# The opening of a two-layer trunk kernel: the first tile scaled behind its transpose, three requests and one rounding in another order

## What is computed

```
def rms_norm(x, g):
    y = x * lax.rsqrt(jnp.mean(x * x, axis=-1, keepdims=True) + EPS)
    return y * g

for l in range(DEPTH):
    h = rms_norm(x, norm_g[l])
    proj = jnp.einsum('bsd,de->bse', h, w_in[l])
    (a_u, a_v, a_z, b_q, b_k, b_v, b_z, i_q, i_k, i_w, g_a, g_b) = split_columns(proj)
    ...
    qi = apply_rope(i_q.reshape(b, s, IDX_HEADS, IDX_DIM), cos_i, sin_i)
    ki = apply_rope(i_k[:, :, None, :], cos_i, sin_i)[:, :, 0, :]
    ...
```

## Time and profile before

| | us |
|---|---|
| median of 3 runs | 775.14 (774.41 to 775.39) |
| the profiled execution | 773.44 |
| its span, first to last instruction | 771.6 |
| TensorE / DVE / ScalarE busy | 762.0 / 620.5 / 460.7 |

### The profile page before, as it was taken

How to read it: one execution, slowest core, us unless ns; L and a number is a source line. 1 busy time by engine, 2 the same in 40 slices (tenths; PEclk the granted TensorE clock), 3 DMA queues, 4 the chain that set the end, 5 groups by cost and what they waited for, 6 DMA issues and landing times.

```text
span 771.6 us, 12228 instructions
## 1 busy us (share of the span) xinstructions
PE 762.0 (99%) x4364; PEld 666.3 (86%) x4364; DVE 620.5 (80%) x1051; ACT 460.7 (60%) x866; POOL 131.5 (17%) x125
## 2 busy tenths in 40 slices
PE   7999999999999999999999999999999999999998
PEld 7988878888899889988899788888889998999886
DVE  5767999999978884689986689999998878746895
ACT  5578786442577556735665977664335684676342
POOL 1344111000030103012215420300011101210130
PEclk9999999999999999999999999999999999999999
DMA  9838558522695529495874745893248844665784
GB/s 330 289 73 200 130 117 227 183 85 83 164 205 148 133 68 156 137 273 127 192 242 148 173 106 149 172 263 110 67 87 221 179 158 69 123 136 181 203 151 122
DMA packets 57900, 123.10 MB, mean 160 GB/s; under 512 B 3824, under 2 KB 8112, under 8 KB 57840
## 3 DMA queue, kind: packets, MB, share of 16 engines
q0 software_dynamic: 23568, 50.42, 34.6%
q1 hardware_dynamic: 33984, 71.31, 28.3%
q10 hardware_dynamic: 288, 0.59, 0.2%
HBM read 107.63 MB, written 10.49 MB: 153 GB/s over the span
## 4 chain that ended last, share of the span: by engine, by line
PE 89%; DVE 4%; ACT 4%; issue 2%; DMA 1%; ACTq 0%; DVEq 0%
PE bank L950 11%; PE bank L952 11%; PE bank L951 11%; PE bank L1020 7%; PE bank L1021 7%; PE bank L1019 7%; PE bank L1103 6%; PE bank L989 3%; PE bank L987 3%; PE bank L988 3%; PE bank L1048 3%; PE bank L1049 3%; PE bank L1050 3%; PE bank L924 2%; PE bank L942 2%
## 5 line engine op out<-in xcount | busy, mean ns | idle before, releaser
L1618 DVE TENSOR_TENSOR w_lo<-w_raw,w_hi 128x1024 fp32r<-128x1024 f32 x168 | 203.1, 1220 | 30.3 <-ACT w_hi L1190 25.4
L1190 ACT ACTIVATE w_hi<-w_raw 128x1024 fp32r<-128x1024 f32 x168 | 172.9, 1052 | 43.4 <-DMA w_raw<-in_w_out 18.9
L783 POOL DMA_DIRECT2D w_raw<-in_w_in x48 | 57.5, 1211 | 396.2 <-DVE w_lo L1618 371.5
L1019 PE MATMUL bank<-h_hi,w_lo 128*128 128x256 f32 x256 | 75.6, 295 | 0.0
L950 PE MATMUL bank<-h_lo,w_hi 128*128 128x512 f32 x192 | 75.5, 393 | 0.0
L952 PE MATMUL bank<-h_hi,w_hi 128*128 128x512 f32 x192 | 74.8, 389 | 0.0
L951 PE MATMUL bank<-h_hi,w_lo 128*128 128x512 f32 x192 | 74.7, 389 | 0.0
L1021 PE MATMUL bank<-h_hi,w_hi 128*128 128x256 f32 x256 | 72.4, 283 | 0.0
L1020 PE MATMUL bank<-h_lo,w_hi 128*128 128x256 f32 x256 | 72.4, 283 | 0.0
L1019 PE MATMUL bank<-hs,w_lo 128*128 128x256 f32 x192 | 56.3, 293 | 0.0
L1698 DVE MAX8 top<-score 128x8 f32<-128x256 f32 (+2 forms) x96 | 53.5, 558 | 3.4 <-DVE g_a L1863 1.8
(11 more groups left out here) (239 smaller groups left out, 1960.9 us busy)
## 6 DMA issues: line engine op xcount, KB each, us to landing
w_raw<-in_w_in SPq DMA_DIRECT2D x84, 512.0 KB, 4.5
w_raw<-in_w_in POOLq DMA_DIRECT2D x48, 512.0 KB, 6.7
w_raw<-in_w_out POOLq DMA_DIRECT2D x16, 512.0 KB, 6.7
w_raw<-in_w_out SPq DMA_DIRECT2D x12, 512.0 KB, 4.3
out<-x_sb POOLq DMA_DIRECT2D x4, 1024.0 KB, 5.8
w_raw<-in_w_oa SPq DMA_DIRECT2D x8, 512.0 KB, 3.7
w_raw<-in_w_ob SPq DMA_DIRECT2D x8, 512.0 KB, 4.1
x_sb<-out POOLq DMA_DIRECT2D x2, 2048.0 KB, 10.9
```

What stands on the lines that cost most here:

```text
L783: pool.dma_start(w_raw[:, slot], block_weights(layer, u), accum_op=ALU.add) \
L1019: nc.tensor.matmul(dst, w_lo[:, wk, col], a_hi[:, k], start=first and i == 0, stop=False, skip_group_check=True)
L1190: nc.scalar.activation(hi, w_raw[:, raw_slot(layer, u)], ACT.Copy).then_inc(s_whi.sem, 1)
L1618: nc.vector.tensor_tensor(lo, w_raw[:, raw_slot(layer, u)], hi.bitcast(F32), ALU.subtract) \
```

## The change

The first tile of layer 0 is no longer multiplied by the norm gain before its transpose. DVE multiplies it by the reciprocal root alone, in two halves with a signal each. The gain stands, transposed, in eight new columns beside the identity matrix (eye_g, whose load grows from 128 to 136 columns) and is applied behind the transpose, where a column of it is a scale per partition: in ScalarE's rounding, now four activations of 128 columns for each half, and in DVE's remainder, four instructions for each half. These transposes go to banks 1 to 4, two blocks in each, and the products of the first tile wait for each k step's remainder alone. norm_bc is requested by ScalarE behind the first tile's root instead of at its start. SP requests the second x tile behind unit 2 instead of ahead of it. POOL requests the rope tables and gains when the second xn is written. ScalarE rounds unit 2 ahead of the second tile's statistics, and DVE takes unit 2's remainder ahead of the second xn and the second half of h_lo ahead of the small weights. In layer 0 the second tile's transposes move from k = 4 to k = 6 of the first tile's products. WARM_UP goes from 18 to 14. In layer 1 only POOL's request is moved.

```diff
@@ constants
-WARM_UP = 18
+WARM_UP = 14
-X_AFTER = {2: [1], 4: [2], 5: [3]}
+X_AFTER = {3: [1], 4: [2], 5: [3]}
@@ tiles
-        eye = sb("eye", [P, P])
+        eye_g = sb("eye_g", [P, P + KD])
+        eye, g_col = eye_g[:, 0:P], eye_g[:, P:P + KD]
@@ POOL
-                pool.wait_ge(s_xn.sem, s_xn.at(layer, 1))
+                pool.wait_ge(s_xn.sem, s_xn.at(layer, 2))
                 pool.dma_start(rope[:], rope_cs).then_inc(s_rope.sem, 16)
@@ TensorE, transpose_x
-                pe.wait_ge(s_xn.sem, s_xn.at(layer, t + 1))
+                first = layer == 0 and t == 0
+                if not first:
+                    pe.wait_ge(s_xn.sem, s_xn.at(layer, t + 1))
...
-                    dst = bank[3 + 2 * (t % 2) + half]
+                    if first:
+                        pe.wait_ge(s_xnhalf, half + 1)
                     for k in range(4):
                         kk = 4 * half + k
-                        last = nc.tensor.transpose(dst[:, k * P:(k + 1) * P], xn[:, t % 2, kk * P:(kk + 1) * P], eye[:])
+                        if first:
+                            dst, col = bank[1 + kk // 2], k % 2 * P
+                        else:
+                            dst, col = bank[3 + 2 * (t % 2) + half], k * P
+                        last = nc.tensor.transpose(dst[:, col:col + P], xn[:, t % 2, kk * P:(kk + 1) * P], eye)
@@ TensorE, index_job
                     for k in ks:
-                        if k % (KD // 2) == 0:
+                        if t == 0 and layer == 0:
+                            pe.wait_ge(s_lo0, k + 1)
+                        elif k % (KD // 2) == 0:
                             pe.wait_ge(s_hlo.sem, s_hlo.at(layer, 2 * t + k // (KD // 2) + 1))
-                        if k == KD // 2 and t + 1 < TILES:
+                        if k == (ks[0] if ks[-1] == KD - 1 and t == layer == 0 else KD // 2) and t + 1 < TILES \
+                                and (layer or t or ks[-1] == KD - 1):
                             transpose_x(layer, t + 1)
@@ ScalarE
-            act.dma_start(eye[:], ident).then_inc(s_eye, 16)
-            act.dma_start(norm_bc[:], norm_g[0]).then_inc(s_norm0, 16)
+            act.dma_start(eye_g[:], ident).then_inc(s_eye, 16)
@@ ScalarE, h_rounded
                     act.wait_ge(s_xt.sem, s_xt.at(layer, 2 * t + half + 1))
+                    if layer == 0 and t == 0:
+                        act.wait_ge(s_eye, 16)
+                        for k in range(4):
+                            kk = 4 * half + k
+                            nc.scalar.activation(h_hi[:, kk, ORDER[0] * P:(ORDER[0] + 1) * P],
+                                                 bank[1 + kk // 2][:, k % 2 * P:(k % 2 + 1) * P], ACT.Copy,
+                                                 scale=g_col[:, kk:kk + 1]).then_inc(s_hi0, 1)
+                        act.wait_ge(s_hi0, 4 * half + 4)
+                        act.sem_inc(s_hhi.sem, 1)
+                        continue
@@ ScalarE, order of the opening
             x_std(0, 0)
+            act.dma_start(norm_bc[:], norm_g[0]).then_inc(s_norm0, 16)
...
                     small_rounded(layer)
+                    rounded(layer, 2)
                     x_std(layer, 1)
-                if layer == 0:
-                    rounded(layer, 2)
                 rounded(layer, 3)
@@ DVE, h_remainder
                 for half in halves:
+                    if layer == 0 and t == 0:
+                        dve.wait_ge(s_eye, 16)
+                        for k in range(4):
+                            kk, tok = 4 * half + k, slice(ORDER[0] * P, (ORDER[0] + 1) * P)
+                            dve.wait_ge(s_hi0, kk - kk % 2 + 2)
+                            nc.vector.scalar_tensor_tensor(h_lo[:, kk, tok], bank[1 + kk // 2][:, k % 2 * P:(k % 2 + 1) * P],
+                                                           g_col[:, kk:kk + 1], h_hi[:, kk, tok].bitcast(F32),
+                                                           ALU.mult, ALU.subtract).then_inc(s_lo0, 1)
+                        dve.wait_ge(s_lo0, 4 * half + 4)
+                        dve.sem_inc(s_hlo.sem, 1)
+                        continue
@@ DVE, first_tile
-                dve.wait_ge(s_norm if layer else s_norm0, 16)
-                x_normalised(layer, 0)
+                if layer:
+                    dve.wait_ge(s_norm, 16)
+                    x_normalised(layer, 0)
+                    return
+                c = 2 * TILES * HEADS
+                dve.wait_ge(s_xstd.sem, s_xstd.at(0, 1))
+                vec.link(dve, nc.vector.reciprocal(rstd[:, c:c + 1], std[:, c:c + 1]))
+                for half in range(2):
+                    cols = slice(half * W512, (half + 1) * W512)
+                    nc.vector.tensor_scalar(xn[:, 0, cols], x_sb[:, ORDER[0], cols], rstd[:, c:c + 1], None,
+                                            ALU.mult).then_inc(s_xnhalf, 1)
+                dve.wait_ge(s_xnhalf, 2)
+                dve.sem_inc(s_xn.sem, 1)
@@ DVE, order of the opening
                     remainder(layer, 1)
+                    h_remainder(layer, 0, [1])
                     small_remainder(layer)
-                    h_remainder(layer, 0, [1])
-                if layer == 0:
+                    remainder(layer, 2)
+                    dve.wait_ge(s_norm0, 16)
                     x_normalised(layer, 1)
-                    remainder(layer, 2)
                 remainder(layer, 3)
@@ host
+    ident = np.concatenate([np.eye(P, dtype=np.float32), np.asarray(norm_g)[0].reshape(KD, P).T], axis=1)
```

## The result

The changed kernel took 774.93 us (median of 22 runs, 772.72 to 777.38). Beside it the kernel before took 773.65 (22 runs, 772.85 to 776.56); the ratio is 1.0016, with a 95% interval of 1.0009 to 1.0022. The change made the kernel **1.2 us slower**. The time lies inside the predicted range, but only because before stood at 775.14 in the three runs the prediction started from; counted from 773.65, the whole range would end at 774.1. The predicted step, 0.9 us faster (a ratio of 0.9988), is outside the interval.

A forecast was written before the change was run, and what follows sets the result against it. TensorE bounds the kernel, busy 762.05 of 771.6 us; only 5.3 idle us at the start can be won. Terms: -1.8 (start) + 0.8 (ScalarE's four) + 0.1 (DVE, TensorE) = -0.9, so 775.14 becomes 774.2 us; range 773.2 to 775.6.

The forecast's parts named there:

- Transposes at 7.9: TensorE's opening: the first tile's transposes start at 7.9 instead of 9.71, 1.8 us early.
- Four activations 1.12, unit 1 at 9.9: ScalarE: four 128-column roundings take 1.12 us, so unit 1's rounding starts at 9.9 instead of 10.92.
- Four remainders 1.16: DVE: the second half's four remainder instructions take 1.16 us, bounds 0.69 and 1.4.
- Third x tile at 16.1 to 16.4, not binding: ScalarE: third x tile lands by 16.1 or 16.4; statistics finish at 17.8, 0.45 us before wanted.
- Tables' product ended by 26.3: POOL's cosine product ends at 26.3, DVE adds it at 28.0: slack 1.7 us, cost zero.
- 0.1 for the wait on the last: DVE: waiting for the last of the four remainders before the small weights' remainder costs 0.1 us.
- 24 took 3.23 us: TensorE: 24 products ahead of the second tile's transposes take 3.23 us, so these start at 17.55.
- the rounding forecast at 18.25: ScalarE rounds the second tile at 18.25 instead of 19.14, a gain of 0.9 us.
- Rival 3: TensorE's opening: the thinned stretch makes the clock fall, half pace for 5.3 us; net 1.7 us slower, 776.9; chance 0.07.
- Rival 4: Tables land over 1.7 us later than forecast and DVE waits, each us beyond costing one; 775 to 776; chance 0.05.
- -1.8 (start): Term of the sum: the first tile's transposes start 1.8 us earlier.
- DVE's tight row carries it to the end: DVE's unbroken work from 19.76 passes the 0.9 us gain to the rotated tile's transposes and the kernel's end.

The follow-up runs named there:

- e2: Changed kernel with the warm-up back at 18 products instead of 14; ratio to before 1.0037.
- e9: Changed kernel with GpSimd's wait for the two norm gains moved behind its first cosine product; ratio to before 1.0015.
- e1: Changed kernel with 16 extra zero products of 128 columns where TensorE stood still in the opening; ratio to before 1.0015.
- e3: Kernel before with only POOL's request for rope tables and gains moved to when the second xn is written; ratio to before 1.0001.
- e4: Changed kernel with DVE taking the small weights' remainder ahead of the second half of h_lo again; ratio to before 1.0015.
- e8: Changed kernel with 16 small zero products added and the tables' request put back behind the first xn; ratio to before 1.0017.
- e6: Kernel before with tables requested at the second xn and POOL's wait for the gains moved behind its first cosine product; ratio to before 0.9988.
- e10: Changed kernel with the gains' wait behind the first cosine product and 4 zero products of 512 columns in the opening; ratio to before 0.9988.
- e11: Kernel before with 16 zero products of 128 columns added in TensorE's opening and nothing else; ratio to before 1.0014.
- e7: Kernel before with a warm-up of 14 products instead of 18 and nothing else; ratio to before 0.9997.

## Why the prediction was wrong, point by point

- **Transposes at 7.9:** 8.02. **Four activations 1.12, unit 1 at 9.9:** 1.14 and 10.03. **Four remainders 1.16:** 1.12 or 1.13 us. **Third x tile at 16.1 to 16.4, not binding:** right in kind, and earlier still, since ScalarE did not wait at 16.14. **Tables' product ended by 26.3:** 26.15. These steps stand.
- **"0.1 for the wait on the last"** remainder was mis-sized. DVE waited 0.57 us for its own fourth instruction before the small remainder (bracket of its row), so that ended at 14.71 instead of 14.25, 0.46 late. Alone it would have left half of the 0.9 us.
- **"24 took 3.23 us"** is the step that failed. It took a duration at full clock into a stretch where the clock fell. They took 4.93 at a granted clock of 0.50 for 3.42 us: 1.70 us more. From 14.35 the products start at 14.77 (0.42) and last 1.70 longer; less 0.14, nearly all of it the overlap of the transposes, which start at 19.53, with the products' end, this is the 1.98 between the rounding forecast at 18.25 and the one found at 20.23.
- **Rival 3** was the right mechanism, with its sign, and had a chance of 0.07. The prediction set against it that before had a similar pause and full clock. The two stretches were not alike: 2.59 busy us in 4.8 there, 2.35 in 5.97 here. And one profiled execution at full clock was no proof: of the 29 runs of before in the first batch 7 had a mean clock of 0.998 or less (a fall of 3.4 us makes 0.998), though no trace shows where in the kernel it fell. Its price was put at 5.3 us of half clock; it was 3.42 in this execution, 6.83 in e2's and e9's.
- **Rival 4** counted only whether the tables land in time. Lateness inside that slack moves GpSimd's product onto other DVE instructions. In the changed kernel this was harmless, since DVE was late as well; in e1, e3 and e4 it cost 1.1 to 1.2 us.
- **"-1.8 (start)"** names the smaller source of the gain. With the tables asked for where before asks, all the rest of the change, clock held, is worth 0.26 us at 30 us (e8); the tables' request with the early cosine product is worth 1.32 without any of it (e6). The earlier landing of the third x tile, which the prediction checked only as a condition, is where most of the gain lies.
- **"DVE's tight row carries it to the end"** held for the changed kernel's delay: +0.90 at 30 us, +1.07 at the last DVE instruction. It does not hold in general. e6 and e10, 1.3 and 1.4 us ahead at 372, were at +0.05 and -0.33 at 398 in their profiled executions. In both the last weight unit of layer 0 landed as late as in before (ScalarE took it up at 378.74 and 378.34; 378.58 in before) although GpSimd asked for it 1.3 us earlier. Nor is it only a lead that goes there: e2, e4 and e11, late at 372 already, lose 1.08, 0.89 and 0.78 us more at the same seam, while the changed kernel, e7 and e9 lose less than 0.1. What holds this unit back was not tried, and stays open; it is as large as all that the change was to gain.

With the clock and the clash both away, the kernel gains about what was forecast: e10 is 1.41 us ahead at 30 us, and 0.9 us faster by the ratio (0.9988; the medians are 773.06 and 773.71). But e6, before with the tables asked for one xn later and the cosine product freed of the gains, is 1.32 us ahead at 30 us and gives the same 0.9988 with one wait changed and one moved. So no run shows that the rearranged first tile is worth anything beside these two waits. e6 and e10 have the lowest ratios here.

## What to carry to other kernels

Before TensorE's work is thinned or pushed later, look at the mean clock of several runs of the old kernel and not of one; where some of them have lost it already, price the work behind the new pause at half pace. Whatever moves an instruction of GpSimd in time is to be checked against each DVE instruction with two SBUF inputs that it can now meet. And count the instructions that an edit adds to an engine: they move the later fetches of its code, and one that lands on a transfer that is waited for cost 0.5 to 0.9 us here, as much as the edit was to gain.

## What the runs showed of the hardware

- **The clock's rise is not tied to the program.** With the same warm-up, records of the zero products stand 0.21 us apart until 7.6 us in the changed kernel and until 6.1 in e1_fill, and 0.11 apart from then on. Over all the profiled executions the change came between 5.5 and 8.1 us. (The clock column of the windows says 1.00 for the warm-up too, included; there the distance tells.) With 14 warm-up products this moves the first transposes (8.02 and 7.30 us), and the changed kernel waits for them. The Trainium skill, "TensorE: Matmul & The Clock Gate", section "Part 1: The HAM clock gate", says that the number of slow products at the start differs from run to run; these runs agree.
- **A fall lasts 3.4 or 6.8 us** in the executions that were profiled, and in the 6.83 us of e9 TensorE was busy for 5.99. The same kernel shows both: e9 has the changed kernel's TensorE program and fell for 6.83 us, the changed kernel itself for 3.42.
- **A DVE wait for its own last instruction** cost 0.57 us, and ScalarE's for its own 0.17 and 0.18.
- **A DVE instruction with two SBUF inputs beside GpSimd's product** takes about twice its time: 1.22 to 2.43 us, 1.28 to 2.42. The one that started first kept its time: in e3 the product (1.43 us, xn 2.42), in e1 xn (1.29 us, the product 2.49).
- **A fetch of code can delay a weight unit** by 0.5 to 0.9 us, 480 us behind the instructions that were added.
